# Rotary embedding of a two-layer kernel: the half swap as transfers inside SBUF instead of TensorE products

## The chip, the cores and the metric

The kernel runs on one core of a Trainium2 chip. The metric is the device time of one execution in microseconds; times inside an execution are those of the profiler, from the start of its span.

## What is computed

Two transformer layers run one after the other on 256 tokens of width 1024, all in float32. The first has a pooling branch, a stick-breaking attention and a cross attention, then a feed-forward. The second projects the normed tokens to queries, keys and values of two attentions (here called a and b), to index queries `qi` and one index key `ki`, to index weights and to two gates. The index scores pick 64 keys per query for attention b. A mixture of 32 experts follows. Queries, keys, `qi` and `ki` are rotated by position before they are used:

```python
def rope(x):
    ...
    x1, x2 = jnp.split(x.astype(jnp.float32), 2, axis=-1)
    return jnp.concatenate([x1 * cos - x2 * sin, x1 * sin + x2 * cos], axis=-1).astype(x.dtype)
```

The two halves of a head of 64 channels are 32 channels each. In the kernel channels lie on partitions, two heads on 128 partitions, so `x2` must come to the partitions of `x1` and the other way round.

## The kernel before, in words

The dense work is cut into **units**: 256 columns of a weight matrix, 8 chunks of 128 rows. SyncE loads unit u into a ring of three slots (L532) once slot u-3 is free. ScalarE rounds the weights to a high part `w_hi` (L1091, waiting until TensorE has finished unit u-3), VectorE subtracts to get the low part `w_lo` (L1349), and TensorE runs 48 products for the unit, high by high, low by high, high by low (L687 to L689), into one of two PSUM banks in turn. A bank is taken again only when the unit before in it has been copied out.

The order of the work on every engine is one list, `step_plan`, which each engine walks through and does its own part of. In the stage of the change it goes through the units kiwi (index key and index weights), qi0, qi1, kb0, kb1, qb0, qb1, vb0, vb1, ka0, ka1, qa0, qa1, va0, va1 and then eight gate units. Eleven of them are **roped**: kiwi, qi, kb, qb, ka, qa. The steps beside the units:

- **unit u.** TensorE: the products. ScalarE: the copy of the result out of PSUM (`evacuate`; for roped units L1137 into `prob_b[r % 2]`, after a wait at L1136 for an earlier rotation, because the buffer is used again), then `w_hi` of unit u+3. VectorE: `w_lo` of unit u+2.
- **rope r, u** (L945 to L952, L1526 to L1534). TensorE multiplies the copied unit by a 128x128 matrix of 1 and -1 (L951), which swaps the halves of each head and turns a sign. VectorE multiplies the copy by the cosine table (L1531), the product by the sine table (L1533), and adds (L1534).
- **index i** (two heads per step). TensorE: scores of index heads i and i+1 (L960, L961). The first such step waits until three rotations are done, and head i waits until the relu of head i-2 is done. ScalarE: relu (L1275), after the `w_hi` of the unit. VectorE: weighted sum (L1691, L1693).
- **topk.** VectorE finds the eight largest of each row and strikes them out (L1700, L1701), eight times. **select** then turns the struck places into a mask (L1703, L1704).
- **heads.** The attentions, pipelined over three steps: scores, middle (transposed weights), values. VectorE takes the maxima (L1460), ScalarE the exponents (L1175), VectorE rescales (L1499), TensorE transposes (L849). The first heads step waits for all eleven rotations. Attention b, which needs the mask, starts with the fifth step.

Rotations, index steps and top-key steps are placed relative to the units: rotation r follows in the step of the next unit, the index steps stand at units 4 to 7 of the stage, the top-key steps from unit 8 on, the last one and the selection at the first gate unit.

Behind this stage the merge, the output product and the experts follow. Expert weights stream through SyncE's queue; their first loads wait for heads that TensorE has finished (L577, L583) and for merged units.

Of the kernel before, what the change touches and what calls it, by code (L numbers as in the profile page):

```python
# [31 lines left out]
P = 128  # L32
# [33 lines left out]
def make_table():  # L66

    t = np.zeros((P, TABLE_W), np.float32)

    def put(name, value):  # L70
        a, b = TABLE[name]
        t[:, a:b] = value

    i, j = np.arange(P)[:, None], np.arange(P)[None, :]
    put("ident", i == j)
    put("later", i > j)
    put("before", i < j)
    rot = np.zeros((P, P), np.float32)
    for p in range(P):
        if p % DH < DH // 2:  # L80
            rot[p + DH // 2, p] = -1.0
        else:
            rot[p - DH // 2, p] = 1.0
    put("rotate", rot)
    put("keep", np.concatenate([i < j, np.ones((P, P)), i < j], 1))
    put("hide", np.where(np.concatenate([j <= i, np.ones((P, P), bool), j <= i], 1), 0.0, NEG))
    inv = np.power(np.float32(10000.0), -np.arange(0, DH, 2, dtype=np.float32) / np.float32(DH))
    ang = (np.arange(T, dtype=np.float32)[None, :] * inv[np.arange(P) % (DH // 2)][:, None]).astype(np.float32)
    put("cos", np.tile(np.cos(ang), (1, 2)))
    put("sin", np.tile(np.sin(ang), (1, 2)))  # L90
    put("slot", np.arange(SLOTS)[None, :])
    put("rev", EXPERTS - np.arange(EXPERTS)[None, :])
    put("revg", GROUPS - np.arange(GROUPS)[None, :])
    put("steps", SLOTS * np.arange(8)[None, :])
    return t
# [74 lines left out]
def step_plan(units):  # L170

    first = {}
    for u, unit in enumerate(units):
        first.setdefault(unit["name"], u)
    plan = []
    ropes = 0

    def unit(u):
        plan.append(("unit", u))

    plan.append(("norm", 0))
    unit(0)
    unit(1)
    plan.append(("norm", 1))
    for u in range(2, 11):
        unit(u)
        if u < 7:
            plan.append(("memory", u - 3))
        if u == 4:
            plan.append(("pool_window",))  # L190
    plan.append(("pool_mix",))
    for k in range(12):
        unit(first["gate"] + k)
        if k % 2:
            plan.append(("heads", *([x, x + 1] if x >= 0 else [] for x in (k - 1, k - 3, k - 5))))
    plan.append(("sigmoid", 0, [(0, j) for j in range(4)]))
    start = first["merge"]
    for n in range(12):
        unit(start + n)
        if n == 0:  # L200
            plan.append(("heads", [], [10, 11], [8, 9]))
        elif n == 1:
            plan.append(("heads", [], [], [10, 11]))
        if n < 4:
            plan.append(("sigmoid", 0, [(1, n), (2, n)]))
        if n in (6, 8):
            plan.append(("finish", n // 2 - 3))
    plan += [("finish", 2), ("finish", 3)]
    for u in range(first["out"], first["out"] + 4):
        unit(u)  # L210
    plan.append(("residual", 0))
    plan.append(("ffn",))
    plan.append(("residual", 1))
    waiting = []
    for u in range(first["kiwi"], first["gate2"]):
        unit(u)
        n = u - first["kiwi"]
        if n == 1:
            plan.append(("row", 3))
        if waiting:  # L220
            plan.append(("rope", *waiting.pop()))
        if units[u]["name"] in ROPED:
            waiting.append((ropes, u))
            ropes += 1
        if 4 <= n < 8:
            plan.append(("index", 2 * (n - 4)))
        if n >= 8:
            plan.append(("topk", n - 8))
    assert not waiting
    for k in range(8):  # L230
        unit(first["gate2"] + k)
        if k == 0:
            plan.append(("topk", 7))
            plan.append(("select",))
        pairs = ([12 + 2 * x, 13 + 2 * x] if 0 <= x < 8 else [] for x in (k, k - 1, k - 2))
        plan.append(("heads", *pairs))
    plan.append(("sigmoid", 1, [(0, j) for j in range(4)]))
    start = first["gate2"] + 8
    unit(start)
    plan.append(("heads", [], [26, 27], [24, 25]))  # L240
    plan.append(("sigmoid", 1, [(1, 0)]))
    unit(start + 1)
    plan.append(("heads", [], [], [26, 27]))
    plan.append(("sigmoid", 1, [(1, 1)]))
    for u in range(start + 2, start + 12):
        unit(u)
        if u < start + 4:
            plan.append(("sigmoid", 1, [(1, u - start)]))
        if start + 5 < u < start + 8:
            plan.append(("finish", u - start - 6))  # L250
        if u == start + 7:
            plan += [("finish", 2), ("finish", 3)]
        if u > start + 8:
            plan.append(("route", u - start - 9))
    plan.append(("route", 3))
    return plan


def layers_kernel(nc, a, table, windows, out):
# [166 lines left out]
    def sem(name):  # L426
        return nc.alloc_semaphore(name)
# [21 lines left out]
                         "right_ready", "o_done", "pair_out"))  # L449
    merged_ready = sem("merged_ready")  # L450
    act_hi, act_ready = sem("ffn_act_hi"), sem("ffn_act_ready")
    rot_done, rope_done, wi_T = sem("rot_done"), sem("rope_done"), sem("wi_out")
    ix_z, ix_relu, ix_acc = sem("index_z"), sem("index_relu"), sem("index_acc")
    act_chain, dve_chain = sem("act_chain"), sem("dve_chain")
    ones_ready = sem("ones_ready")
# [226 lines left out]
    def _(pe):  # L682
# [198 lines left out]
        for step, *arg in plan:  # L881
# [57 lines left out]
            elif step == "ffn":  # L939
                unit(G0)  # L940
                row(2)
                unit(G0 + 1)
                ffn_loop(pe, triple)
                unit(S2 + 3 * (NF - 1))
            elif step == "rope":  # L945
                r, u = arg
                wait_out(pe, u)
                if r >= 1:
                    pe.wait_ge(rope_done, r)
                n = T if r == 0 else 2 * T  # L950
                mm(ps[:, 7, 0:n], const("rotate"), prob_b[r % 2][:, 0:n], start=True, stop=True)\  # L951
                    .then_inc(rot_done, 1)  # L952
            elif step == "index":
                pe.wait_ge(rope_done, 3)
                for i in (arg[0], arg[0] + 1):
                    p0 = DH * (i % 2)
                    q, kk, bank = qi[p0:p0 + DH, i // 2, :], ki[p0:p0 + DH, :], 4 + i % 2
                    if i >= 2:
                        pe.wait_ge(ix_relu, i - 1)
                    mm(ps[:, bank, 0:P], q[:, 0:P], kk[:, 0:P], start=True, stop=True)  # L960
                    mm(ps[:, bank, P:CAUSAL], q[:, P:T], kk, start=True, stop=True).then_inc(ix_z, 1)  # L961
            elif step == "route":
                r = arg[0]
                if r:
                    route_logits(r - 1)
                pe.wait_ge(hg_ready, r + 1)
                for tb in range(TB):
                    for c in range(2):
                        last = nc.tensor.transpose(ps[:, 2 + r, T * c + P * tb:T * c + P * tb + P],
                                                   n3[:, tb, UC * r + P * c:UC * r + P * c + P], ident)  # L970
                last.then_inc(route_T, 1)
            elif step == "memory":
                if arg[0] == 0:
                    row(1)
            elif step in ("finish", "topk", "select", "sigmoid"):
                pass
            else:
                raise ValueError(step)
# [79 lines left out]
    def _(act):  # L1058
# [44 lines left out]
        copies = {"mk": mk, "q": q1, "k": k1, "xq": xq}  # L1103
        tokens = {"mv": mv, "p": p_tok, "v": v1, "vb": vb, "va": va}

        def evacuate(u):

            x = units[u]
# [20 lines left out]
            elif name == "kiwi":  # L1129
                act.wait_ge(sq_done, 4)  # L1130
                link(fn(score_b[0][0:8, 0:T], full[0:8, T:2 * T], ACT.Copy, scale=512.0 ** -0.5))
                fn(prob_b[0][:, 0:T], full[:, 0:T], ACT.Copy).then_inc(out_act, 1)
            elif name in ROPED:
                r = rope_of[u]
                if r >= 2:
                    act.wait_ge(rope_done, r - 1)  # L1136
                fn(prob_b[r % 2][:, :], full, ACT.Copy).then_inc(out_act, 1)  # L1137
            else:
                raise ValueError(name)

# [188 lines left out]
    def _(dve):  # L1329
# [196 lines left out]
        def rope(r, u):  # L1526
# [2 lines left out]
            name = units[u]["name"]  # L1529
            dst = ki[:, :] if r == 0 else flat(roped[name][:, 2 * units[u]["j"]:2 * units[u]["j"] + 2, :])  # L1530
            link(v.tensor_tensor(expo_b[s][:, 0:n], prob_b[s][:, 0:n], const("cos")[:, 0:n], ALU.mult))  # L1531
            dve.wait_ge(rot_done, r + 1)
            link(v.tensor_tensor(right_b[s][:, 0:n], ps[:, 7, 0:n], const("sin")[:, 0:n], ALU.mult))  # L1533
            v.tensor_tensor(dst, expo_b[s][:, 0:n], right_b[s][:, 0:n], ALU.add).then_inc(rope_done, 1)  # L1534

        def ffn():
# [333 lines left out]
```

## Time and profile before

| | |
|---|---|
| median of 3 runs | 1137.14 us (1136.83 to 1137.33) |
| profiled execution | 1136.4 us, span 1134.6 us |
| TensorE busy | 944.4 us, 83% |
| VectorE busy | 527.2 us, 46% |
| ScalarE busy | 361.9 us, 32% |
| matrix-engine clock, mean granted | 0.943 |
| DMA | 310.03 MB, mean 273 GB/s |

Busy shares are means over stages with different limits. In the time line, "idle before <- releaser" stands in brackets behind an instruction that had to wait, with the instruction that ended the wait. ACTq and SPq are the sequencers of ScalarE and SyncE, where transfers are issued. Lines with "x2" merge two instructions that stand next to each other.

### The profile page before, as it was taken

The page shows a single profiled execution, that of the slowest core. Times are in us where ns is not written, and L with a number is a line of the kernel's source. Part 1 is how long each engine was busy: PE and PEld are TensorE (multiplying, and loading weights), DVE is VectorE, ACT ScalarE, POOL GpSimd, SP SyncE. Part 2 cuts the span into 40 slices and gives each one's busy share as a digit, 9 for nine tenths or more (in the row PEclk, how much of TensorE's full clock was granted, in tenths as well). Part 3 has the DMA queues.
Part 4 walks back from the last instruction along what each step waited for, and adds up shares of the span by engine and source line. Part 5 has one row for each costly group of instructions (what it writes and reads, how often), then busy time and mean ns, then how long its engine had stood idle before and what let it go on. Part 6 is the DMA issues. An engine that isn't in the chain of part 4 may idle for free.

```text
span 1134.6 us, 23812 instructions
## 1 busy us (share of the span) xinstructions
PE 944.4 (83%) x10517; PEld 831.3 (73%) x10517; DVE 527.2 (46%) x856; ACT 361.9 (32%) x541; POOL 46.4 (4%) x43
## 2 busy tenths in 40 slices
PE   8999999899999998999999897756565656566663
PEld 7999998899999997989988896545344534444442
DVE  4545766766655655778876742212120212121212
ACT  4544555454333335343666431100010100000001
POOL 0100001400000000000210200000000000000000
PEclk9999999999999999999999999979797978898888
DMA  9754413746555543544434988999999999999993
GB/s 338 232 186 144 150 63 115 236 134 217 184 173 200 185 156 120 171 146 155 150 120 153 356 343 362 428 425 430 429 426 430 428 426 430 428 427 429 430 427 148
DMA packets 109521, 310.03 MB, mean 273 GB/s; under 512 B 5684, under 2 KB 92408, under 8 KB 96664
## 3 DMA queue, kind: packets, MB, share of 16 engines
q1 hardware_dynamic: 107712, 304.66, 69.7%
q0 software_dynamic: 1008, 4.20, 1.0%
q8 instruction: 44, 0.72, 0.2%
q10 hardware_dynamic: 744, 0.35, 0.1%
q14 instruction: 13, 0.11, 0.0%
HBM read 308.14 MB, written 1.05 MB: 273 GB/s over the span
## 4 chain that ended last, share of the span: by engine, by line
PE 53%; issue 41%; DVE 3%; ACT 1%; POOL 1%; DMA 0%; ACTq 0%; POOLq 0%; DVEq 0%
PE ps L687 16%; PE ps L689 16%; PE ps L688 16%; PE ps L951 1%; DVE w_lo L1349 1%; PE ps L861 1%; PE ps L849 0%; DMA rows<-in_g_mix 0%; PE ps L790 0%; PE ps L839 0%; DVE x_f L1390 0%; PE ps L828 0%; PE ps L827 0%; DVE h L1439 0%; POOL stat L633 0%
## 5 line engine op out<-in xcount | busy, mean ns | idle before, releaser
L687 PE MATMUL ps<-x_hi,w_hi 128*128 128x256 f32 x928 | 266.3, 287 | 0.0
L688 PE MATMUL ps<-x_lo,w_hi 128*128 128x256 f32 x928 | 262.4, 283 | 0.0
L689 PE MATMUL ps<-x_hi,w_lo 128*128 128x256 f32 x928 | 262.4, 283 | 0.0
L1026 PE MATMUL ps<-arena,xg 128*32 128x128 f32 x3968 | 141.2, 305 | 68.1 <-DMA arena<-in_w 62.0
L1349 DVE TENSOR_TENSOR w_lo<-arena,w_hi 128x2048 fp32r<-128x2048 f32 (+3 forms) x83 | 166.3, 2007 | 52.8 <-ACT w_hi L1091 52.2
L1026 PEld LDWEIGHTS ps<-arena,xg 128*32 128x32 f32 x3968 | 124.5, 123 | 89.2 <-DMA arena<-in_w 77.3
L687 PEld LDWEIGHTS ps<-x_hi,w_hi 128*128 128x128 f32 x928 | 176.9, 191 | 5.4 <-issue 4.3
L688 PEld LDWEIGHTS ps<-x_lo,w_hi 128*128 128x128 f32 x928 | 177.0, 191 | 1.6 <-issue 1.0
L689 PEld LDWEIGHTS ps<-x_hi,w_lo 128*128 128x128 f32 x928 | 177.0, 191 | 0.2
L1091 ACT ACTIVATE w_hi<-arena 128x2048 fp32r<-128x2048 f32 (+3 forms) x83 | 138.6, 1671 | 40.8 <-PE ps L689 27.7
L1036 PE MATMUL ps<-arena,hid_T 128*32 128x256 f32 x992 | 75.2, 455 | 60.1 <-DMA arena<-in_w 47.3
L1805 DVE TENSOR_TENSOR hid<-silu_e,ps 128x128 f32<-128x128 f32 x32 | 11.9, 371 | 196.8 <-ACT silu_e L1312 196.8
L1036 PEld LDWEIGHTS ps<-arena,hid_T 128*32 128x32 f32 x992 | 35.2, 126 | 91.4 <-issue 51.7
L687 PE MATMUL ps<-w_hi,x_hi 128*128 128x256 f32 x256 | 75.7, 296 | 8.8 <-DVE w_lo L1349 7.0
L1813 DVE COPY y_quad<-ps 32x256 f32<-32x256 f32 x64 | 27.2, 425 | 106.6 <-PE ps L1036 105.6
L689 PE MATMUL ps<-w_hi,x_lo 128*128 128x256 f32 x256 | 73.8, 288 | 0.0
L688 PE MATMUL ps<-w_lo,x_hi 128*128 128x256 f32 x256 | 73.7, 288 | 0.0
L1359 DVE TENSOR_TENSOR w_lo<-arena,w_hi 128x2048 fp32r<-128x2048 f32 x24 | 55.0, 2293 | 31.2 <-ACT w_hi L1101 31.2
L1312 ACT ACTIVATE silu_e<-ps 128x128 f32<-128x128 f32 x32 | 8.9, 278 | 186.7 <-PE ps L1026 186.7
L1315 ACT ACTIVATE y_quad<-ps 32x256 f32<-32x256 f32 x64 | 23.9, 374 | 130.3 <-PE ps L1036 129.5
L1101 ACT ACTIVATE w_hi<-arena 128x2048 fp32r<-128x2048 f32 x24 | 45.9, 1911 | 49.9 <-PE ps L689 49.9
L687 PEld LDWEIGHTS ps<-w_hi,x_hi 128*128 128x128 f32 x256 | 50.6, 198 | 11.2 <-DVE w_lo L1349 7.6
(269 smaller groups left out, 1318.8 us busy)
## 6 DMA issues: line engine op xcount, KB each, us to landing
arena<-in_w SPq DMA_DIRECT2D x90, 2048.0 KB, 25.7
arena<-in_w_in SPq DMA_DIRECT2D x43, 1024.0 KB, 5.1
arena<-in_w_ffn_in SPq DMA_DIRECT2D x22, 1024.0 KB, 5.0
arena<-in_w_ffn_out SPq DMA_DIRECT2D x11, 1024.0 KB, 4.8
arena<-in_w_out SPq DMA_DIRECT2D x8, 1024.0 KB, 7.6
arena<-in_w SPq DMA_DIRECT2D x6, 1024.0 KB, 9.6
third_w<-in_w SPq DMA_DIRECT2D x3, 2048.0 KB, 12.6
arena<-in_w_mem_kv SPq DMA_DIRECT2D x2, 1024.0 KB, 5.3
```

The costliest lines, as they stand in the source:

```text
L687: mm(dst, l_hi, r_hi, start=start, stop=False)
L688: mm(dst, l_hi, r_lo, start=False, stop=False)
L689: return mm(dst, l_lo, r_hi, start=False, stop=stop)
L1026: last = mm(ps[SLOTS * g:SLOTS * g + SLOTS, 4 + e % 2, P * n:P * n + P], xg[:, c, SLOTS * e:SLOTS * e + SLOTS], places[n][:, c, P * g:P * ...
L1036: last = mm(ps[SLOTS * g:SLOTS * g + SLOTS, 7, 0:UC], hid_T[:, SLOTS * b:SLOTS * b + SLOTS], places[2][:, b, UC * g:UC * g + UC], start=b ...
L1091: fn(w_hi[:, u % 3, 0:n], ring[:, u % 3, 0:n], ACT.Copy).then_inc(hi_ready, 1)
L1101: fn(w_hi[:, s, :], ring[:, s, :], ACT.Copy).then_inc(hi_ready, 1)
L1315: fn(y_quad[SLOTS * e:SLOTS * e + SLOTS, UC * g:UC * g + UC], ps[SLOTS * g:SLOTS * g + SLOTS, 7, 0:UC], ACT.Copy).then_inc(e_yA, 1)
L1349: v.tensor_tensor(w_lo[:, u % 3, 0:n], ring[:, u % 3, 0:n], w_hi[:, u % 3, 0:n].bitcast(F32), ALU.subtract).then_inc(lo_ready, 1)
L1359: v.tensor_tensor(w_lo[:, s, :], ring[:, s, :], w_hi[:, s, :].bitcast(F32), ALU.subtract)\
L1805: v.tensor_tensor(hid[:, :].rearrange("p (b i) -> p i b", b=4), silu_e[:, :].rearrange("p (i b) -> p i b", b=4), ps[:, 4 + e % 2, P:2 * P] ...
L1813: v.tensor_copy(y_quad[SLOTS * e:SLOTS * e + SLOTS, UC * g:UC * g + UC], ps[SLOTS * g:SLOTS * g + SLOTS, 7, 0:UC]).then_inc(e_yD, 1)
```

## The change

The rotation product disappears from TensorE. When ScalarE has copied a roped unit into `prob_b[s]`, it waits until the copy is complete and issues four transfers, each of 32 partitions and up to 2 KB per partition, from `prob_b[s]` to `right_b[s]` with neighbouring blocks of 32 partitions exchanged. The sign moves into the sine table. VectorE waits for the four landings and multiplies `right_b[s]` by the table in place. In the plan a rotation now follows two units behind its own unit instead of one, the index steps stand at units 5 to 8, the top-key steps from unit 9 on, the last two at the first two gate units, and the selection at the second.

```diff
-    put("sin", np.tile(np.sin(ang), (1, 2)))
+    sign = np.where(np.arange(P) % DH < DH // 2, np.float32(-1.0), np.float32(1.0))[:, None]
+    put("sin", np.tile(np.sin(ang), (1, 2)) * sign)
...
-        if waiting:
-            plan.append(("rope", *waiting.pop()))
+        if waiting and waiting[0][1] == u - 2:
+            plan.append(("rope", *waiting.pop(0)))
         if units[u]["name"] in ROPED:
             waiting.append((ropes, u))
             ropes += 1
-        if 4 <= n < 8:
-            plan.append(("index", 2 * (n - 4)))
-        if n >= 8:
-            plan.append(("topk", n - 8))
+        if 5 <= n < 9:
+            plan.append(("index", 2 * (n - 5)))
+        if n >= 9:
+            plan.append(("topk", n - 9))
     assert not waiting
     for k in range(8):
         unit(first["gate2"] + k)
-        if k == 0:
-            plan.append(("topk", 7))
+        if k < 2:
+            plan.append(("topk", 6 + k))
+        if k == 1:
             plan.append(("select",))
...
-            elif step == "rope":
-                r, u = arg
-                wait_out(pe, u)
-                if r >= 1:
-                    pe.wait_ge(rope_done, r)
-                n = T if r == 0 else 2 * T
-                mm(ps[:, 7, 0:n], const("rotate"), prob_b[r % 2][:, 0:n], start=True, stop=True)\
-                    .then_inc(rot_done, 1)
...
+        def turn_halves(u, n):
+
+            s = rope_of[u] % 2
+            act.wait_ge(out_act, outs(u, False))
+            for b in range(4):
+                at_b, from_b = slice(32 * b, 32 * b + 32), slice(32 * (b ^ 1), 32 * (b ^ 1) + 32)
+                act.dma_start(right_b[s][at_b, 0:n], prob_b[s][from_b, 0:n]).then_inc(turned[s], 16)
...
                 fn(prob_b[0][:, 0:T], full[:, 0:T], ACT.Copy).then_inc(out_act, 1)
+                turn_halves(u, T)
             elif name in ROPED:
                 r = rope_of[u]
                 if r >= 2:
                     act.wait_ge(rope_done, r - 1)
                 fn(prob_b[r % 2][:, :], full, ACT.Copy).then_inc(out_act, 1)
+                turn_halves(u, 2 * T)
...
             link(v.tensor_tensor(expo_b[s][:, 0:n], prob_b[s][:, 0:n], const("cos")[:, 0:n], ALU.mult))
-            dve.wait_ge(rot_done, r + 1)
-            link(v.tensor_tensor(right_b[s][:, 0:n], ps[:, 7, 0:n], const("sin")[:, 0:n], ALU.mult))
+            dve.wait_ge(turned[s], 64 * (r // 2 + 1))
+            link(v.tensor_tensor(right_b[s][:, 0:n], right_b[s][:, 0:n], const("sin")[:, 0:n], ALU.mult))
             v.tensor_tensor(dst, expo_b[s][:, 0:n], right_b[s][:, 0:n], ALU.add).then_inc(rope_done, 1)
```

## Rows read from the trace of the kernel before

**Rows 1.** The chain that ended last, 440 to 620 us, shares by line.

```profile
by line: PE ps L687 26.1%; PE ps L688 24.8%; PE ps L689 24.7%; PE ps L951 5.1%; PE ps L849 3.1%; PE ps L861 2.3%; PE ps L828 1.9%; PE ps L827 1.9%; PE ps L961 1.0%; PE ps L960 1.0%; ACT head_prob L1175 1.0%; ACT gates L1251 0.9%; issue 0.9%
```

**Rows 2.** The same chain in order of time: start us, us, what.

```profile
469.07 0.86 PE ps L951 x2
475.68 0.86 PE ps L951 x2
...
483.35 0.86 PE ps L951 x2
...
565.17 0.81 PE ps L849 x6
```

**Rows 3.** Time line of ScalarE: start us, us, instruction [idle before <- releaser].

```profile
455.47 0.60 ACT L1137 ACTIVATE head_prob<-ps 128x512 f32<-128x512 f32 x1 [3.16 <-PE ps L689]
...
491.54 1.91 ACT L1091 ACTIVATE w_hi<-arena 128x2048 fp32r<-128x2048 f32 x1
493.35 0.87 ACT L1275 ACTIVATE head_score<-ps 128x384 f32<-128x384 f32 x2
...
512.64 1.90 ACT L1091 ACTIVATE w_hi<-arena 128x2048 fp32r<-128x2048 f32 x1
```

**Rows 4.** Time line of VectorE, an index step and a rotation with top-key step.

```profile
493.86 1.78 DVE L1693 SCALAR_TENSOR_TENSOR score<-head_score,index_w,score 128x128 f32<-128x128 f32 x4 [0.47 <-ACT head_score L1275]
495.68 2.29 DVE L1349 TENSOR_TENSOR w_lo<-arena,w_hi 128x2048 fp32r<-128x2048 f32 x1
...
514.64 2.29 DVE L1349 TENSOR_TENSOR w_lo<-arena,w_hi 128x2048 fp32r<-128x2048 f32 x1 [1.50 <-ACT w_hi L1091]
516.85 0.68 DVE L1531 TENSOR_TENSOR head_expo<-head_prob,tab 128x512 f32<-128x512 f32 x1
518.83 0.69 DVE L1533 TENSOR_TENSOR head_right<-ps,tab 128x512 f32<-128x512 f32 x1 [1.30 <-PE ps L951]
519.56 0.69 DVE L1534 TENSOR_TENSOR ka<-head_expo,head_right 128x512 f32<-128x512 f32 x1
520.17 0.29 DVE L1700 MAX8 best<-work 128x8 f32<-128x128 f32 x1
...
521.86 2.29 DVE L1349 TENSOR_TENSOR w_lo<-arena,w_hi 128x2048 fp32r<-128x2048 f32 x1
```

**Rows 5.** Time line of ScalarE's queue at the start, three of seven issues.

```profile
1.23 0.57 ACTq L1073 DMA_DIRECT2D rows<-in_norm_mem  x1
1.83 0.28 ACTq L1073 DMA_DIRECT2D rows<-in_norm_mix_pre  x1
...
3.35 0.41 ACTq L1075 DMA_DIRECT2D pool_w_sb<-in_w_pool_mix  x1
```

**Rows 6.** DMA issues of the whole run: KB each, median us to landing.

```profile
arena<-in_w_in SPq DMA_DIRECT2D x43, 1024.0 KB, 5.1
...
pool_w_sb<-in_w_pool_mix ACTq DMA_DIRECT2D x1, 256.0 KB, 6.9
```

**Rows 7.** Instructions of line 1534, the one of half width.

```profile
L1534 DVE TENSOR_TENSOR ki<-head_expo,head_right x1: 425/425/425, 459.3 to 459.3; 128x256 f32<-128x256 f32 x1
```

**Rows 8.** Time line of VectorE and ScalarE, selection and first heads step.

```profile
551.12 1.16 DVE L1703 TENSOR_SCALAR score<-work 128x384 f32<-128x384 f32 x1
...
552.90 0.29 DVE L1460 CUSTOM_DVE_ANT_0 head_score<-ps,tab 128x128 f32<-128x128 f32 x1
...
553.91 0.40 ACT L1175 ACTIVATE head_prob<-head_score,softmax 128x128 f32<-128x128 f32 x1
...
555.07 0.17 DVE L1496 RECIPROCAL softmax<-softmax 128x2 f32<-128x2 f32 x1 [0.32 <-ACT head_prob L1175]
...
556.29 0.68 DVE L1499 TENSOR_SCALAR head_prob<-head_prob,softmax 128x128 f32<-128x128 f32 x2
```

**Rows 9.** TensorE in stretches: busy us (instructions), granted clock, DMA share, GB/s.

```profile
636.00:640.00 4.00, 0.98 (x6) 1.00 1.06 365
640.00:644.00 4.00, 3.73 (x18) 0.57 1.03 380
```

More of the change, by code:

```diff
@@ L451, in layers_kernel @@
     act_hi, act_ready = sem("ffn_act_hi"), sem("ffn_act_ready")
-    rot_done, rope_done, wi_T = sem("rot_done"), sem("rope_done"), sem("wi_out")
+    turned, rope_done, wi_T = [sem("turned0"), sem("turned1")], sem("rope_done"), sem("wi_out")
     ix_z, ix_relu, ix_acc = sem("index_z"), sem("index_relu"), sem("index_acc")
@@ L974, in _ @@
                     row(1)
-            elif step in ("finish", "topk", "select", "sigmoid"):
+            elif step in ("finish", "rope", "topk", "select", "sigmoid"):
                 pass
```

## The prediction

> **What bounds the kernel now.** I first asked which engine carries the stage of the change, with the chain that ended last cut to 440 to 620 us. Nearly all of it is TensorE; the rotation products (L951) alone are 5.1% of 180 us, 9.2 us, and all lie on the chain [rows 1]. The same chain in order of time gives TensorE's beat: 6.61 us from one rotation to the next, 0.86 of it the rotation, so 5.75 for a unit's 48 products; with an index step the beat is 7.67, so that step costs 1.06 [rows 2]. In other words, here TensorE waits for nobody, and what leaves its queue is a gain as long as nobody else becomes slower than 5.75 us per unit. The next question is therefore what ScalarE and VectorE need per unit, and above all **in which order they need each other**. The time line of each gives durations [rows 3, 4]. ScalarE: copy of a unit out of PSUM 0.60, then the high part w_hi 1.91, from whose start VectorE's w_lo can start 2.00 later. VectorE: w_lo 2.21, cosine product 0.73, sine product 0.73, sum 0.69 (0.61 until the next instruction starts), one top-key step 1.69. That is 5.92 per unit with its 1.30 wait taken out, already more than 5.75.
>
> **What the order of the code makes of it.** Today rotation r of unit u is done while unit u+1 runs. The copy of a roped unit waits for the rotation before the last one (L1136), which then had a whole unit to spare. Now rotation r is done in unit u+2's step, behind w_lo of unit u+4, and the copy in that same step waits for it. This closes a ring over two engines: copy of unit u, four transfer issues, w_hi of u+3, w_lo of u+3, rotation of u-1, and only then copy of u+1. The issues stand on ScalarE's queue in front of w_hi, and cannot start before the copy is complete.
>
> **Removed.** 22 recorded matmuls (11 full-precision products), 9.2 us on the path [rows 1]; their cover is none, so alone this is -9.2. VectorE's sine product reads SBUF instead of PSUM: the cosine product, which reads SBUF now, takes 0.68 against 0.69 [rows 4], so nothing.
>
> **Added: 44 transfers on ScalarE's queue.** The trace has no transfer inside the chip, so I bound the issue. Behind each other on this queue issues took 0.28 to 0.57; the last five stand 0.39 apart on average (1.83 to 3.76) [rows 5]. I take 0.40, so 1.60 per rotation; ends 0.28 and 0.57. The Trainium skill (DMA: Bandwidth & Descriptors, "Issuing engines are not separate DMA queues") says that the sequencer's time to start a transfer "is usually small relative to the DMA itself"; by it the 1.60 would be near nothing and the kernel would take about 1133. That is a rival below. The landing: 256 KB on this queue took 6.9 us at the crowded start, a 1 MB weight load 5.1 in the median [rows 6]. The sine product comes 10 us or more after the last issue (the first rotation has the least: kiwi's copy is a unit of 5.75 before qi0's at 455.47, its issues are over by about 452, and its sine product comes at about 462.4 by the sum below), so I count nothing; beyond 10 us it would be the next thing late. The weight loads share the engines with 256 KB per rotation; a load takes 5.1 and its slot is free two units ahead, so nothing.
>
> **The ring.** 0.62 (copy, seen complete) + 1.60 + 2.00 + 2.21 + 0.73 + 0.73 + 0.75 (sum, seen) = **8.64 us against TensorE's 5.75**. With an index step it is worse, for ScalarE does the relus behind w_hi (1.81 later) and VectorE, in order, waits for them (0.51 later) and adds 1.82 before its next w_lo [rows 3, 4]. Stock: TensorE starts about two units ahead of need, so the delay shows late. I follow it in times of the trace, from the copy of qi0 at 455.47 [rows 3]; up to there kiwi's issues delay only w_hi of kb0, which is not needed for two units:
> - + 0.62 + 1.60 + 2.00 + 2.21 + 1.37 (kiwi's rotation, three instructions of half width, 0.425 and a gap each [rows 7]) = 463.27, copy of qi1
> - + 3 rings, 25.92 = 489.19, copy of qb0
> - + 0.62 + 1.60 + 1.81 + 0.51 + 1.82 + 2.21 + 2.21 = 499.97, copy of qb1
> - + 0.62 + 1.60 + 1.81 + 0.90 (both relus) = 504.90. TensorE's third index step waits for these relus (its second had waited too).
> - TensorE: three units and two index steps, 19.37, and 0.20 of drain = 524.47, copy of ka1
> - + 2 rings, 17.28 = 541.75, copy of qa1
> - + 4.22 (copy, issues, w_hi) + w_lo 2.21, rotation 2.07, top-key 1.69, w_lo 2.21, rotation 2.07 = 556.22: the last rotation, for which the heads wait.
>
> Now the moved steps come in, all on VectorE. + 1.69 + 2.21 + 1.69 (two top-key steps around a w_lo) = 561.81. From the maxima 1.01 to the exponent, 1.16 to the rescaling, 1.81 to the end of both heads' [rows 8] = 565.79. Then w_lo 2.21, top-key 1.69, selection 1.78, 1.01, 1.16, and 1.56 until the second head's weights are there (1.96, less the first head's transposes, 0.40) = 575.20. TensorE's same step began at 565.17 [rows 2]. From there on TensorE has been the slower one again, and what follows is released by it: the weights of the experts included. So the end moves by 575.20 - 565.17 = **+10.0 us**, with the 9.2 saved already in it. TensorE's waits should sum to some 19.
>
> The profiled execution took 1136.4 with a span of 1134.6; the median is 1137.14, 0.7 above. I add 10.0 to the median: **1147.1**. The chain holds nine groups of four issues, so each 0.01 per issue is worth 0.36: at 0.28 the result is +5.7 (1142.8), at 0.57 +16.1 (1153.3). The other terms stand nine times too; 0.1 wrong per ring is 0.9.
>
> **TensorE's clock.** It idles about 7 us at the second index step and 4 at the third. When it had been busy only 0.98 of 4 us, the next 4 us were granted 0.57 [rows 9], that is, mostly the lower level (1.2 GHz). 3.4 us at that level would lose 1.7. The lost time falls into the following wait for the ring, so I count nothing, up to 1.7 above.
>
> **Rivals.** A measurement of this kernel can tell about 0.2%, 2.3 us, from no change.
> - *Cheap issues.* If an issue costs ScalarE little, the ring is 7.04 plus the rest, still over 5.75, but only the shortened waits remain. Place: between copy and w_hi. The sum breaks even at 0.12 per issue and reaches about 1133 at nothing. For it: none of the present issues is inside the chip. Against: seven rows, none under 0.28. Chance 0.10, of which 0.04 is faster by over 2.3 and 0.06 within it.
> - *No ring, the whole gain.* If the copy's wait were always over already, the 9.2 would land: 1127.9. This decides the sign if VectorE reaches the rotation before TensorE ends the unit. Against: w_lo cannot start before 0.62 + 2.00 us after the copy, plus 2.21 and 2.21, is 7.04 even without issues, above 5.75. Chance 0.04.
> - *Late landings.* The small transfers queue behind 1 MB loads and take over 10 us; at 12 us each sine product waits about 2 and the chain grows by about 4: 1151. For it: the DMA engines are also busy with weights. Against: 6.9 is the longest comparable row. Chance 0.08.
> - *As forecast*, ring with issues of 0.28 to 0.57: 0.76. A last 0.02 is for no visible change from causes I don't see.
>
> **Numbers.** Slower 0.76 + 0.08 = 0.84; same 0.06 + 0.02 = 0.08; faster 0.04 + 0.04 = 0.08. The likeliest case's own range is 1142.8 to 1153.3. The low end is taken down to 1139, issues near 0.18, halfway to the cheap ones; the high end up to 1156, late landings or a lost clock on top of dear issues.
>
> **What would show it.** Right: ScalarE's copy of a roped unit no longer waits for TensorE, but some 4 to 5 us for VectorE's rotation sum, in qi1, kb0, kb1, qb0, qb1, qa0, qa1; copies of those are about 8.6 apart; four issues of 0.4 between copy and w_hi; TensorE idle before index steps two and three (about 7 and 4 us), and about 2 to 3 before the first scores and the first two middles. Wrong: waits of the copy on TensorE as now; issues of 0.1; a sine product that waits for DMA; or, if the beat of TensorE stays near 5.75 through 456 to 544 us, the ring itself.

## The result: 1162.3 us, slower by 2.2%, and the profile after

The changed kernel took 1162.29 us in the median of four runs (1162.09 to 1165.89), the kernel before 1137.02 (1136.83 to 1137.33) beside it. The ratio is 1.0224, with a 95% interval of 1.0207 to 1.0241: +25.3 us where +10.0 was forecast. Run once more later, it took 1164.68 us against 1138.4, a ratio of 1.0233 (1.0213 to 1.0253). The profiled execution is the longest of the four, 1165.89 us with a span of 1164.1. One of the ten executions of experiment 4 took 1165.33 us at a granted clock of 0.815, where the other nine had 0.933 to 0.944; it enters no comparison.

From the page of the kernel after, the first line, two groups of instructions (busy us, mean ns | idle before, releaser), and two kinds of transfer (KB each, us to landing):

```profile
span 1164.1 us, 23802 instructions
L1353 DVE TENSOR_TENSOR w_lo<-arena,w_hi 128x2048 fp32r<-128x2048 f32 (+3 forms) x83 | 166.3, 2007 | 82.0 <-ACT w_hi L1085 81.5
L1085 ACT ACTIVATE w_hi<-arena 128x2048 fp32r<-128x2048 f32 (+3 forms) x83 | 138.5, 1671 | 69.2 <-issue 30.1
...
arena<-in_w_in SPq DMA_DIRECT2D x43, 1024.0 KB, 5.5
...
head_right<-head_prob ACTq DMA_DIRECT2D x40, 64.0 KB, 2.7
```

The idle time in front of `w_lo` was 52.8 us before and is 82.0, that in front of `w_hi` 40.8 and now 69.2. The small transfers land after 2.7 us: they are not late. The weight loads went from 5.1 us [rows 6] to 5.5. Next, the chain of the kernel after, 440 to 620 us (what [rows 1] showed before), shares by line, cut after the twelfth by the view itself:

```profile
by line: issue 14.5%; ACTq L1106 12.6%; PE ps L689 10.2%; PE ps L690 9.4%; PE ps L691 9.3%; ACT w_hi L1085 8.6%; DVE head_right L1537 3.4%; DVE head_expo L1535 3.3%; ACT head_prob L1140 3.0%; DVE w_lo L1353 2.8%; ACT head_prob L1179 2.2%; D
```

TensorE's three product lines held 75.6% of this stretch [rows 1] and hold 28.9% now. The transfer issues at L1106 alone hold 12.6% of 180 us, 22.7 us: work that moves nothing itself, on the path nine times. The time line of ScalarE and its queue shows one turn of the ring (start us, us, instruction [idle before <- releaser]):

```profile
485.21 0.60 ACT L1140 ACTIVATE head_prob<-ps 128x512 f32<-128x512 f32 x1 [4.47 <-DVE qi L1538]
485.83 2.44 ACTq L1106 DMA_DIRECT2D head_right<-head_prob  x4
488.38 1.92 ACT L1085 ACTIVATE w_hi<-arena 128x2048 fp32r<-128x2048 f32 x1 [2.57 <-issue]
494.77 0.60 ACT L1140 ACTIVATE head_prob<-ps 128x512 f32<-128x512 f32 x1 [4.47 <-DVE kb L1538]
```

and VectorE's time line has its other half:

```profile
490.32 2.29 DVE L1353 TENSOR_TENSOR w_lo<-arena,w_hi 128x2048 fp32r<-128x2048 f32 x1 [5.21 <-ACT w_hi L1085]
492.53 0.69 DVE L1535 TENSOR_TENSOR head_expo<-head_prob,tab 128x512 f32<-128x512 f32 x1
493.25 0.69 DVE L1537 TENSOR_TENSOR head_right<-head_right,tab 128x512 f32<-128x512 f32 x1
493.98 0.69 DVE L1538 TENSOR_TENSOR kb<-head_expo,head_right 128x512 f32<-128x512 f32 x1
```

Read the two together: copy 485.21, issues, `w_hi` 488.38, `w_lo` 490.32, rotation 492.53 to 494.67, next copy 494.77. A turn takes 9.56 us where a unit costs TensorE 5.75. Both engines idle in it, each for the other: that is the mark of a ring, and busy shares hide it. The sine product L1537 follows the cosine product without a gap, so it never waits for a landing.

The waits of the kernel after, 440 to 640 us (us in total, times, longest), give the sizes:

```profile
DVE w_lo L1353 <- ACT w_hi L1085: 37.1, 10, 5.5
ACT w_hi L1085 <- issue: 30.1, 11, 3.4
...
ACT head_prob L1140 <- DVE kb L1538: 10.2, 2, 5.7
...
ACT head_prob L1140 <- DVE ka L1538: 9.1, 2, 4.5
ACT head_prob L1140 <- DVE qi L1538: 8.9, 2, 4.5
PE ps L954 <- ACT head_score L1279: 8.9, 2, 6.8
...
ACT head_prob L1140 <- DVE ki L1538: 3.7, 1, 3.7
```

Copies wait 32.0 us in all (seven times) for rotation sums; in the kernel before, these copies waited for TensorE alone. To measure the stage by itself I take two landmarks that every version has: the first accumulator read of the last norm, and the table load before the second layer's sigmoids, which follows the last exponents. In the kernel after:

```profile
445.72 0.20 ACT L1148 ACTIVATION_READ_ACCUMULATOR junk<-h 128x1 f32 x1
...
637.65 1.28 ACT L1255 ACT_TABLE_LOAD   x1
```

and in the kernel before:

```profile
445.76 0.20 ACT L1144 ACTIVATION_READ_ACCUMULATOR junk<-h 128x1 f32 x1
...
612.03 1.28 ACT L1251 ACT_TABLE_LOAD   x1
```

The **stage** is thus 191.9 us long after and 166.3 before: +25.6. The routing behind it, from this table load to the next, in front of its exponent, is 64.5 in both. So nearly the whole loss lies in the stage of the change.

### The profile page after: what moved, and what is told of

The parts are those of the page before. It is cut to its first block, busy times and chain, and to the rows that moved or that the text cites. A ratio compares the mean times of both kernels' runs of the same rounds, so it can differ in the third digit from the quotient of the medians.

```text
span 1164.1 us, 23802 instructions
## 1 busy us (share of the span) xinstructions
PE 947.5 (81%) x10495; PEld 834.8 (72%) x10495; DVE 528.7 (45%) x856; ACT 362.8 (31%) x541; POOL 45.7 (4%) x43
## 4 chain that ended last, share of the span: by engine, by line
PE 44%; issue 42%; DVE 6%; ACT 3%; ACTq 2%; POOL 1%; DMA 0%; POOLq 0%; DVEq 0%
PE ps L689 14%; PE ps L690 13%; PE ps L691 13%; ACTq L1106 2%; ACT w_hi L1085 1%; DVE w_lo L1353 1%; PE ps L863 1%; DVE head_right L1537 1%; DVE head_expo L1535 1%; ACT head_prob L1179 0%; ACT head_prob L1140 0%; DMA rows<-in_g_mix 0%; DVE head_prob L1503 0%; PE ps L792 0%; PE ps L851 0%
## 5 line engine op out<-in xcount | busy, mean ns | idle before, releaser
L1353 DVE TENSOR_TENSOR w_lo<-arena,w_hi 128x2048 fp32r<-128x2048 f32 (+3 forms) x83 | 166.3, 2007 | 82.0 <-ACT w_hi L1085 81.5
L1020 PE MATMUL ps<-arena,xg 128*32 128x128 f32 x3968 | 138.1, 301 | 68.3 <-DMA arena<-in_w 60.5
L1085 ACT ACTIVATE w_hi<-arena 128x2048 fp32r<-128x2048 f32 (+3 forms) x83 | 138.5, 1671 | 69.2 <-issue 30.1
L1030 PEld LDWEIGHTS ps<-arena,hid_T 128*32 128x32 f32 x992 | 35.4, 128 | 93.7 <-issue 58.4
## 6 DMA issues: line engine op xcount, KB each, us to landing
arena<-in_w SPq DMA_DIRECT2D x90, 2048.0 KB, 25.6
```

The lines of the kernel that those rows point to most:

```text
L1020: last = mm(ps[SLOTS * g:SLOTS * g + SLOTS, 4 + e % 2, P * n:P * n + P], xg[:, c, SLOTS * e:SLOTS * e + SLOTS], places[n][:, c, P * g:P * ...
L1030: last = mm(ps[SLOTS * g:SLOTS * g + SLOTS, 7, 0:UC], hid_T[:, SLOTS * b:SLOTS * b + SLOTS], places[2][:, b, UC * g:UC * g + UC], start=b ...
L1085: fn(w_hi[:, u % 3, 0:n], ring[:, u % 3, 0:n], ACT.Copy).then_inc(hi_ready, 1)
L1353: v.tensor_tensor(w_lo[:, u % 3, 0:n], ring[:, u % 3, 0:n], w_hi[:, u % 3, 0:n].bitcast(F32), ALU.subtract).then_inc(lo_ready, 1)
```

## Experiments

Each diff is against the kernel after, unless it says otherwise. Where an experiment puts the placement back, that is the same three edits of the plan.

**1. The placement alone undone** (`e_lag1`), transfers still on ScalarE's queue.

```diff
-        if waiting and waiting[0][1] == u - 2:
+        if waiting:
...
-        if 5 <= n < 9:
-            plan.append(("index", 2 * (n - 5)))
-        if n >= 9:
-            plan.append(("topk", n - 9))
+        if 4 <= n < 8:
+            plan.append(("index", 2 * (n - 4)))
+        if n >= 8:
+            plan.append(("topk", n - 8))
...
-        if k < 2:
-            plan.append(("topk", 6 + k))
-        if k == 1:
+        if k == 0:
+            plan.append(("topk", 7))
```

> The four transfers per rotation stay on ScalarE's queue, but rotation, index and top-key steps go back to where the kernel before has them, one unit after their unit. Ring theory: the copy of a roped unit then waits for a rotation that was finished a unit earlier, so a turn of the ring (9.55 us with the issues of 2.56 that the changed kernel shows) is shared by two units, 4.8 per unit, under TensorE's 5.75; the products are gone from TensorE, so about 8 us faster than the kernel before: 1129, with ScalarE's copies of roped units waiting for TensorE again. Rival, ScalarE's time: eleven times 2.56 us of issues is 28 us on the path, less the 9.2 of the products; then the placement is of no account and the time stays near 1156 to 1162. Rival, landings: with a lag of one unit the sine product would come too early for the 2.7 us of a landing; then 1135 to 1150 with VectorE waiting for DMA at the sine product.

Measured: 1133.27 us (1131.88 to 1139.62), ratio 0.9973 (0.9945 to 1.0001), stage 161.1. The same transfers with the same issues no longer cost; ScalarE's time line shows why:

```profile
472.31 0.60 ACT L1139 ACTIVATE head_prob<-ps 128x512 f32<-128x512 f32 x1 [0.24 <-PE ps L690]
472.94 2.44 ACTq L1105 DMA_DIRECT2D head_right<-head_prob  x4
475.48 1.92 ACT L1084 ACTIVATE w_hi<-arena 128x2048 fp32r<-128x2048 f32 x1 [2.57 <-issue]
```

The copy waits for TensorE again (0.24 us), so issues and `w_hi` are filled into time that ScalarE has. The gain is half of what I expected. The copy had only 0.24 us to spare here, so with four issues ScalarE is nearly the bound; experiment 9 takes them away.

**2. The placement alone made** (`e_plan_only`): the kernel before, products kept, with the plan of after (the diff of experiment 1 turned round).

> The kernel before, products on TensorE and all, with only the plan of the changed kernel: rotations two units after their unit, index, top-key and selection one unit later. Ring theory: the ring is there but without issues, 7.0 us per turn against 6.61 of TensorE with a product in each unit, so about 1 us slower than the kernel before: 1138, the most 1141. If the moved steps were the main loss: 1150 or more. ScalarE's time as the cause: no change, 1137.

Measured: 1142.28 us (1141.09 to 1144.61), ratio 1.0049 (1.0029 to 1.0069), stage 167.7. The ring is there without a single transfer, as two lines of ScalarE's time line show:

```profile
477.71 0.60 ACT L1138 ACTIVATE head_prob<-ps 128x512 f32<-128x512 f32 x1 [4.47 <-DVE qi L1535]
...
484.59 0.60 ACT L1138 ACTIVATE head_prob<-ps 128x512 f32<-128x512 f32 x1 [4.47 <-DVE kb L1535]
```

A turn is 6.88, only 0.27 over TensorE's beat with a rotation, 6.61 [rows 2]. That is why the placement by itself costs the stage only 1.4 us. The median rose by 4.8, though, past the 1141 expected at most: of the 4.7 between the profiled executions 3.2 lie behind the routing, and no run explains them. The experiment also shows that the wait of 4.47 has nothing to do with transfers: it is `w_hi`, `w_lo` and rotation seen from the copy.

**3. A third pair of buffers** (`e_third`), placement of after: the ring is cut, nothing else.

```diff
+    prob_r = [prob_b[0], prob_b[1], spare[0]]
+    right_r = [right_b[0], right_b[1], spare[1]]
...
-                if r >= 2:
-                    act.wait_ge(rope_done, r - 1)
-                fn(prob_b[r % 2][:, :], full, ACT.Copy).then_inc(out_act, 1)
+                if r >= 3:
+                    act.wait_ge(rope_done, r - 2)
+                fn(prob_r[r % 3][:, :], full, ACT.Copy).then_inc(out_act, 1)
```

> The changed kernel with a third pair of buffers for the copy and its turned halves, so that a copy waits for the rotation three before and not two before; everything stays two units late and all issues stay on ScalarE. Ring theory: a turn of the ring is again shared by two units; about 6 to 7 us faster than the kernel before: 1130 to 1131, a little above the kernel with a lag of one, because selection and heads are late. ScalarE's time as the cause: near 1156 to 1162. If the loss came from the moved steps (rotation, index, top-key, selection): no gain from the buffers, 1155 or more.

Measured: 1138.55 us (1134.92 to 1140.05), ratio 1.0006 (0.9996 to 1.0016), stage 164.6. One buffer more takes back 24 of the 25 us, so the reuse of the buffer closes the ring. But I had expected 1130 to 1131. The steps that still come late, index, top-key and selection, show in the waits of 440 to 620 us at the exponents:

```profile
ACT head_prob L1182 <- DVE softmax L1471: 12.1, 8, 4.3
```

In the kernel before this wait was 4.7 us in seven times, in experiment 1 7.7 in eight. Behind it, TensorE waits 3.6 us for rescaled weights, where it waited 1.8 in experiment 1. With about 1.6 of a lower clock in the first unit, which experiment 1 did not have (see below), that makes nearly the 3.5 us between the two stages. The medians lie 5.3 apart; the rest is not explained.

**4. The issues moved away** (`e_on_sp`), placement of after: SyncE issues the four transfers.

```diff
+        def turn_halves(u):
+            s, n = rope_of[u] % 2, T if rope_of[u] == 0 else 2 * T
+            sp.wait_ge(out_act, outs(u, False))
+            for b in range(4):
...
+                sp.dma_start(right_b[s][at_b, 0:n], prob_b[s][from_b, 0:n]).then_inc(turned[s], 16)
...
+            if u - 5 in rope_of:
+                turn_halves(u - 5)
```

> The changed kernel with its plan and two buffers, but the four transfers are issued on SyncE's queue, placed ahead of the weight load five units on. Ring theory: the ring remains without issues, 7.0 us per turn against TensorE's 5.75; by the same sum about 5 us faster than the kernel before, 1132, with TensorE still waiting about 2 us at an index step and about 1 us at the first two middles. If landings or traffic of the transfers were the loss: as slow as the changed kernel, 1155 or more. If the moved steps were the loss: also 1150 or more.

Measured: 1134.69 us in the median of nine runs (1132.59 to 1138.1), ratio 0.9977 (0.9962 to 0.9992); the profiled one took 1134.82. That is 2.8 faster than the kernel before, not 5. Stage 163.2, and ScalarE's time line:

```profile
477.92 0.60 ACT L1149 ACTIVATE head_prob<-ps 128x512 f32<-128x512 f32 x1 [4.47 <-DVE qi L1546]
478.41 1.91 ACT L1095 ACTIVATE w_hi<-arena 128x2048 fp32r<-128x2048 f32 x1
484.79 0.60 ACT L1149 ACTIVATE head_prob<-ps 128x512 f32<-128x512 f32 x1 [4.47 <-DVE kb L1546]
```

The turn is 6.87 again. Transfers and bytes are those of the kernel after; they land after 2.0 us instead of 2.7, but VectorE waited for no landing in either. What the turn has lost is ScalarE's time for the issues, 9.56 - 6.87 = 2.69 us.

**5. Half the transfers** (`e_two`). Only the lower 64 partitions are turned; the upper 64, one head in two, are left out.

```diff
-            for b in range(4):
+            for b in range(2):
...
-            dve.wait_ge(turned[s], 64 * (r // 2 + 1))
+            dve.wait_ge(turned[s], 32 * (r // 2 + 1))
```

> The changed kernel with two of the four transfers per rotation; the lower 64 partitions get their turned halves, the upper 64 keep what lay in the buffer. This leaves out half of the turning. Ring theory with 0.64 us per issue: each turn of the ring is 1.28 us shorter, 8.3 instead of 9.55, and the time falls by about 13 us: 1147 to 1150. If the issues were nothing and the placement all: no change, 1162.

Measured: 1150.39 us (1149.12 to 1151.2), just above the expected range, ratio 1.0111 (1.0096 to 1.0125), stage 176.9.

```profile
471.84 1.16 ACTq L1106 DMA_DIRECT2D head_right<-head_prob  x2
473.10 1.91 ACT L1085 ACTIVATE w_hi<-arena 128x2048 fp32r<-128x2048 f32 x1 [1.29 <-issue]
479.48 0.60 ACT L1140 ACTIVATE head_prob<-ps 128x512 f32<-128x512 f32 x1 [4.47 <-DVE qi L1538]
```

**6. Twice the transfers, the same bytes** (`e_eight`): eight of 16 partitions.

```diff
-            for b in range(4):
-                at_b, from_b = slice(32 * b, 32 * b + 32), slice(32 * (b ^ 1), 32 * (b ^ 1) + 32)
+            for b in range(8):
+                at_b, from_b = slice(16 * b, 16 * b + 16), slice(16 * (b ^ 2), 16 * (b ^ 2) + 16)
...
-            dve.wait_ge(turned[s], 64 * (r // 2 + 1))
+            dve.wait_ge(turned[s], 128 * (r // 2 + 1))
```

> The changed kernel with eight transfers of 16 partitions instead of four of 32; the same bytes and the same result. If an issue costs 0.64 us whatever it moves, each turn of the ring grows by 2.56 to 12.1 us and the kernel by about 27: 1185 to 1195. If the cost goes with partitions or bytes, an issue takes about 0.32 and the time stays at 1162 to 1168.

Measured: 1192.93 us (1190.81 to 1193.83), ratio 1.049 (1.0474 to 1.0505), stage 219.3.

```profile
483.18 5.00 ACTq L1106 DMA_DIRECT2D head_right<-head_prob  x8
488.27 1.92 ACT L1085 ACTIVATE w_hi<-arena 128x2048 fp32r<-128x2048 f32 x1 [5.13 <-issue]
```

From copy to `w_hi` it is 1.29, 2.57 and 5.13 us for two, four and eight transfers: 0.64 each, whether of 32 partitions or of 16. Turns are 8.27, 9.56 and 12.1, stages 176.9, 191.9 and 219.3: about 11 us of stage for each us of turn.

**7. No transfers, lag of one unit** (`e_copies`). Ahead of its copy of the unit, ScalarE copies it out of PSUM in four blocks of 32 partitions, each to its neighbour's place. Placement as in experiment 1.

```diff
-            act.wait_ge(out_act, outs(u, False))
+            full = ps[:, bank_of[u], :]
...
-                act.dma_start(right_b[s][at_b, 0:n], prob_b[s][from_b, 0:n]).then_inc(turned[s], 16)
+                ins = fn(right_b[s][at_b, 0:n], full[from_b, 0:n], ACT.Copy)
+                ins.then_inc(turned[s], 1)
```

> Steps placed as in the kernel before (lag of one unit), no transfers: ScalarE writes the turned halves itself, by four copies of 32 partitions from PSUM to the neighbouring block, before it copies the unit. Ring theory: no ring; ScalarE has 4 x 0.5 + 0.5 + 1.9 = 4.4 us per unit, 5.3 with an index step, under TensorE's 5.75: about 8 us off the stage, 1129 to 1131, the fastest of all unless the sine product waits. If ScalarE's time as such was the loss: slower than with transfers on another queue, 1135 or more.

Measured: 1132.34 us (1129.04 to 1136.24), 1.3 above the expected range, ratio 0.9957 (0.9944 to 0.997), stage 157.6. The chain from 455 to 600 us, by line:

```profile
by line: PE ps L688 29.5%; PE ps L690 27.9%; PE ps L689 27.9%; PE ps L850 3.9%; PE ps L862 2.4%; PE ps L829 2.4%; PE ps L828 2.4%; PE ps L954 1.2%; PE ps L953 1.2%; PE ps L867 0.9%; PE ps L779 0.3%; PE ps L894 0.1%; issue 0.0%
```

TensorE carries the stage alone, without its rotation products. The stage is 8.7 us shorter, close to the 9.2 of those products [rows 1].

**8. No transfers, lag of two units** (`e_copies_lag2`): the copies of experiment 7 with the placement of after. This decides between "the ring" and "the DMA".

> No transfers at all: ScalarE turns the halves by four copies of 32 partitions (2.43 us together, where the four issues take 2.44), with the plan of the changed kernel, rotations two units late. Ring theory: a turn is about 9.3 us (the unit's copy starts 2.46 late and w_hi 0.49 behind it), nearly the 9.55 of the changed kernel; about 18 us off by the sum for this ring, plus some 3 for TensorE's lower clock after its waits: 1154 to 1160. If transfers are what costs (their issue, their landing, their traffic): as fast as the same copies with a lag of one unit, 1132.

Measured: 1159.9 us (1156.74 to 1161.27), ratio 1.0197 (1.0178 to 1.0217), stage 184.0. ScalarE's time line:

```profile
473.43 2.42 ACT L1106 ACTIVATE head_right<-ps 32x512 f32<-32x512 f32 x4 [4.47 <-DVE qi L1539]
475.88 0.60 ACT L1142 ACTIVATE head_prob<-ps 128x512 f32<-128x512 f32 x1
476.38 1.91 ACT L1085 ACTIVATE w_hi<-arena 128x2048 fp32r<-128x2048 f32 x1
482.75 2.43 ACT L1106 ACTIVATE head_right<-ps 32x512 f32<-32x512 f32 x4 [4.47 <-DVE qi L1539]
```

A turn of 9.32 us and most of the loss, without one transfer. 2.4 us of ScalarE's time inside the ring cost this, as copies or as issues.

**9. SyncE's queue, lag of one unit** (`e_sp_lag1`): experiments 1 and 4 together.

> The four transfers on SyncE's queue and steps placed as in the kernel before (lag of one unit). Ring theory: neither ring nor issues on ScalarE; the sine product may wait 0.4 us for a landing, which TensorE doesn't see: about 9 us off the stage, 1129 to 1131. The rival that the transfers lose against the weight loads on the same queue: landings of 5 us or more, waits of VectorE at the sine product, 1135 or more.

Measured: 1132.66 us (1129.51 to 1136.41), ratio 0.9954 (0.9936 to 0.9972), stage 159.3. That is 1.7 above the expected range. Without issues on ScalarE the stage is 1.8 us shorter than in experiment 1, although this execution had a lower clock in its first unit (see below) and that one had not; in the medians the two can't be told apart.

**10. The kernel after, once more** (`e_again`), on the chip of experiment 8.

> The changed kernel once more, beside the kernel before on the same chip, for a second look at its stages. 1162 to 1166; the stage from the last norm to the second layer's sigmoids 25 to 26 us longer than in the kernel before, the stretches behind it equal within 4 us.

Measured: the 1164.68 us named above, with a stage of 192.1. The loss of the whole change repeats.

The stage in us, from the same two landmarks in each trace, puts the experiments in order:

| halves are swapped by | one unit late | two units late | price of the lag |
|---|---|---|---|
| TensorE products | 166.3 (before) | 167.7 | 1.4 |
| transfers, SyncE's queue | 159.3 | 163.2 | 3.9 |
| transfers, ScalarE's queue | 161.1 | 191.9 (after) | 30.8 |
| copies by ScalarE | 157.6 | 184.0 | 26.4 |

The lag is nearly free while ScalarE does nothing new, and the issues are nearly free while the lag is one unit. Together they cost 32.6 over SyncE's queue at one unit, nearly six times the sum of their prices (1.8 for ScalarE's queue at one unit, 3.9 for the lag on SyncE's). The table takes each stage as its one trace has it. The kernel after and both versions on SyncE's queue had the lower clock in the first unit, worth about 1.6 us; the other five had not. With that taken out, the issues at one unit cost about 3.4 instead of 1.8, and the whole is still over four times the sum.

## Why the prediction was wrong in size

**Right: sign, mechanism and place.** The rotation sum releases the copy in just the seven units named. Landings are hidden, the weight loads are hardly touched, TensorE idles before the second and third index steps (6.8 and 2.2 us, where about 7 and 4 were named, and 3.0 before the first, where none was), and the routing behind the stage keeps its 64.5 us. The rivals fell one by one: no cheap issue, no late landing, and a ring in every version with a lag of two units and two buffers. In the stage nearly the whole gain of the removed products does come once the ring is away (experiment 7), but not here.

**Wrong: the term for the issues.** The step was "Behind each other on this queue issues took 0.28 to 0.57 ... I take 0.40, so 1.60 per rotation". Four issues took 2.44 us and, with the way back to ScalarE, 2.57. That is 0.64 per issue, above even the upper bound of 0.57. With 0.64 in place of 0.40 the prediction's own sum would give +18.7, 1155.8 us, just inside its range of 1139 to 1156; the terms below, counted as nothing or missing, took the result out of it. The rows were transfers of other shapes, from HBM, at the start of the run; nothing tied them to a transfer of 32 partitions inside the chip, and the seven rows were a sample, not a limit. The same kernel's weight loads on SyncE's queue (L532) already had issues from 0.37 to 1.31 us. The chain of the kernel after shows one group singly:

```profile
495.39 0.51 ACTq L1106
495.94 0.61 ACTq L1106
496.58 0.61 ACTq L1106
497.22 0.61 ACTq L1106
...
534.38 1.29 ACTq L1106
...
555.59 1.45 ACTq L1106
```

The rest of the sum, walked at the same places (us; the right column is the growth of the error in that step):

| reached | predicted | measured | new error |
|---|---|---|---|
| copy of qi0 | 455.47 | 457.06 | 1.6 |
| copy of qi1 | 463.27 | 465.89 | 1.0 |
| copy of qb0, three turns | 489.19 | 494.77 | 3.0 |
| copy of qb1 | 499.97 | 506.31 | 0.8 |
| both relus | 504.90 | 512.15 | 0.9 |
| copy of ka1 | 524.47 | 533.20 | 1.5 |
| copy of qa1, two turns | 541.75 | 553.13 | 2.6 |
| end of the last rotation | 556.22 | 570.41 | 2.8 |
| weights of the first heads | 565.79 | 581.05 | 1.1 |
| weights of the second heads | 575.20 | 590.59 | 0.1 |

The last measured value is 590.99, the end of the second head's weights, less the 0.40 taken off in the prediction. The errors sum to 15.4, and 10.0 + 15.4 = 25.4 is the stage's 25.6. Of the 15.4:

- **8.6** is the issue time: nine groups, each 2.55 from its first issue to `w_hi`, against 1.60.
- **1.7** are groups of 2.66, 3.12 and 3.28 us instead of 2.44, where single issues stretched (two are in the fence above). The prediction had no term for it. In the trace of experiment 10 the groups of ka1 and qa1 are long too, 3.35 and 2.97.
- **1.6** is the first unit. TensorE's granted clock was low there in this execution. Of the experiments, 3, 4, 9 and 10 had it too (granted 0.50 to 0.62 from 441 to 445 us), 1, 2, 5, 6, 7 and 8 had 1.00, though no edit touches the work before that unit, and experiments 5 and 6 issue transfers in the same places. So this part seems to be the execution's and not the change's. But both traces of the kernel after have it, and its other executions have no trace.
- **2.3** is VectorE beside GpSimd: three instructions lost 0.95, 1.06 and 1.07, and the selection, slowed before, got 0.8 back (see below).
- The last **1.2** is the step to ka1, 1.5, less 0.3 over the other steps. There TensorE was at the lower clock behind its wait for the relus (512 to 516 us below: 20 products, and 35 in the next four us).

**Wrong: the clock counted as nothing.** The stretches of TensorE, first of the kernel after (us, TensorE busy, its weight loads, VectorE, ScalarE, GpSimd, then the granted clock, DMA share, GB/s):

```profile
441.00:445.00 4.00, 3.22 (x14) 2.83 (x15) 3.37 (x10) 2.66 (x8) 0.00 (x0) 0.50 0.14 49
...
492.00:496.00 4.00, 1.58 (x14) 1.38 (x12) 2.60 (x4) 0.60 (x1) 0.00 (x0) 0.93 0.56 159
496.00:500.00 4.00, 0.00 (x0) 0.00 (x0) 0.00 (x0) 2.06 (x2) 0.00 (x0) 0.50 0.56 169
500.00:504.00 4.00, 3.63 (x16) 3.01 (x17) 3.60 (x5) 0.60 (x2) 0.00 (x0) 0.50 0.00 0
...
512.00:516.00 4.00, 4.00 (x20) 3.35 (x20) 3.86 (x6) 3.56 (x6) 0.00 (x0) 0.57 0.00 0
```

then 441 to 445 of the kernel before:

```profile
441.00:445.00 4.00, 2.74 (x22) 2.27 (x22) 3.83 (x11) 3.05 (x9) 0.00 (x0) 1.00 0.20 78
```

In the whole stretch of 440 to 612 us the granted clock was 0.91, in the kernel before 1.00. At 0.50, the level of 1.2 GHz, TensorE did 14 products in 3.22 us; before, at 1.00, 22 in 2.74. In the four us ahead of that, TensorE had been busy the same 2.3 in both kernels, so its own work doesn't tell the two executions apart. Between 492 and 496 it was busy 1.58 us, between 496 and 500 not at all, at the lower level, and the next four were granted that level too. Most of this falls into waits that the ring would have made anyway, as predicted, but not all of it: 1.6 on the first unit, and about 1.5 behind the third index step, where the copies of ka0 and ka1 wait for TensorE (3.27 and 0.67 us) and none waits for the ring.

## What stays open

The stage gains of experiments 1, 4, 7 and 9, 5.2, 3.1, 8.7 and 7.0 us, stand in the medians as 4.2, 2.8, 5.0 and 4.7. The losses are larger in the medians as well: 4.8 against 1.4 in the stage in experiment 2, 1.0 against a gain of 1.7 in experiment 3, 13.0 against 10.7, 55.6 against 53.0 and 21.5 against 17.7 in experiments 5, 6 and 8. So up to 4 us behind the stage go with the version or with the execution, and no run tells which. Part of it is single executions: in that of experiment 9 the time from the last gathering copy (`xg`) to the issue of the last output transfer was 62.6 us, in those of the kernel before and of experiment 7 58.4 and 58.5; the routing took 66.1 instead of 64.5. The same last stretch took 62.7 in the profiled execution of the kernel after, which would account for the 3.6 us that it lies over its median. It varied between 58 and 63 with no edit that could reach it, and what sets it was not tested.

Of the versions run, the copies by ScalarE with a lag of one unit (1132.34 us) and the transfers on SyncE's queue with a lag of one unit (1132.66) are the fastest, 0.4 to 0.5% under the kernel before. They can't be told apart.

## What to carry to other kernels

Before moving a step later, follow its buffer: if the producer's next write waits for the moved step, the delay becomes a ring, and everything that those engines do between the two points sets its turn, however idle they look. Price an added issue on the engine that pays for it, inside that ring and from rows of the same kind of transfer; where none exists, the spread of unlike rows is no bound. And test the two halves of a change apart: here each alone moved the time by half a per cent at most, and together by 2.2%.

## What was not expected of the hardware

- **Issue time goes by the transfer, not by its size.** 0.51 us for the first of a group and 0.61 for the others, 0.64 from one to the next, with 32 partitions or 16, some stretched to 1.29 and 1.45. The engine's next instruction waits for all of it. SyncE's queue took as long, 2.41 us for the four (experiment 4), while the issue of a 1 MB weight load there took 0.37 (median of 45, kernel before). The Trainium skill (DMA: Bandwidth & Descriptors, "Issuing engines are not separate DMA queues") holds that the time to initiate is "usually small relative to the DMA itself". The trace does not bear that out for these transfers: 2.44 us to issue four, 2.7 to land one. With the rule's other half, that another engine's queue saves only that time, experiment 4 agrees: it saved 2.69 us per turn.
- **VectorE stops beside GpSimd.** VectorE and then GpSimd, kernel after:

```profile
568.05 0.69 DVE L1537 TENSOR_TENSOR head_right<-head_right,tab 128x512 f32<-128x512 f32 x1
568.77 1.64 DVE L1538 TENSOR_TENSOR qa<-head_expo,head_right 128x512 f32<-128x512 f32 x1
```

```profile
568.24 1.63 POOL L676 TENSOR_TENSOR gates<-gates,rstd_row 128x512 f32<-128x512 f32 x1 [120.13 <-ACT gates L1130]
579.64 1.27 POOL L676 TENSOR_TENSOR gates<-gates,rstd_row 128x512 f32<-128x512 f32 x1 [9.78 <-ACT gates L1130]
```

The sum that takes 0.69 us elsewhere took 1.64 and ended 0.54 after GpSimd's instruction (569.87). GpSimd's own had begun during the sine product, which kept its 0.69, and took 1.63 against 1.27. The Trainium skill (SBUF — State Buffer, "SBUF: two separate sides") describes a pair of ports that the two engines share under an exclusive lock, held for a whole instruction. The rows agree with it: the loss is a wait until the other's end, not a slower pace. No run took GpSimd's instruction away, so this is argued from the rows.
